# First block's mixing stage: rope on GpSimd, the first long tile's scores evicted by ScalarE, one mask add for all heads

## The chip, the cores and the metric

The kernel runs on one NeuronCore of a Trainium2 chip. The metric is the device time of one execution in microseconds (us). The core's engines take their instructions in order, each from its own queue, and wait for one another through semaphores: TensorE (PE in the profile, its weight loads PEld), VectorE (DVE), ScalarE (ACT), GpSimd (POOL) and SyncE (SP, which issues the DMAs here).

## The reference

Two blocks of two layers each run one after the other. Only the first block is touched. Its residual has 272 positions (16 learned ones and 256 tokens) of width 1024, all in float32. One layer of it is

```
z = x @ w_in                            # 4176 columns
q,k,v -> causal conv of width 4, silu -> gated delta rule, 4 heads of 128
sq,sk,iq,ik = rope(...)                 # rope(x) = x*cos + rot(x)*sin
score = sum_h relu(iq_h . ik / 8) * wi_h, causal     # 8 heads of 64
keep  = the best 64 positions of each row by score
p = softmax(sq_h . sk_h / 8 where kept, else -inf);  o_h = p @ sv_h
x = layer_norm(alpha*x + [delta, sparse] @ w_out);  then a mixture of experts
```

## The kernel before

Activations lie transposed: features on the 128 partitions, the 272 positions along the free axis. For the attention, the queries are cut into tiles of 16, 128 and 128 rows (`TILES`); tile 1 sees 144 keys, tile 2 sees 272. Softmax with kept positions only is made by adding a mask `bias` that is 0 or -1e30.

`mixers` builds one layer's mixing stage out of three parts: `projections` (35 groups of matmuls, the conv and the rope), `delta_rule` (three chunks of 16, 128 and 128 positions; a chunk's triangular inverse goes through up to six levels, each a round from TensorE over ScalarE and VectorE back) and `sparse_attention`. Each part is a generator for each engine, and it yields a planned time ahead of each step. `interleave` merges the three generators of an engine by these planned times. So the planned times (`projection_time`, `DELTA_START`, `RANK_START`, `ATTEND_START`) fix the order of the instructions on each engine and nothing else; the engines then run that order with semaphore waits. Planned times are not microseconds of the profile.

In words, the steps that the change touches:

- **Rope.** ScalarE copies a projection out of its bank (line 278) into `ikT` (1 group of 272 columns), `iqT`, `sqT` and `skT` (4 groups each). When a tensor is whole, `swap(r)` on SyncE issues four DMAs (line 211) that write the halves swapped into `rope_tmp`, which lies in the room of `xT` and is shown by that name. VectorE then does three passes: `swapped *= sin` (317), `x *= cos` (319), `x += swapped` (322), and counts `rope_out`. The next swap waits for it. TensorE waits for `rope_out` 2 ahead of the first ranking matmul (719) and for 4 ahead of the first attention score (737).
- **Ranking.** For each tile, eight heads go from TensorE (719) through a relu on ScalarE (792) to an accumulation on VectorE (845, 847). Then VectorE finds the best 64 in eight rounds (857, 859) and makes the mask (862, 864).
- **Attention.** For each tile TensorE writes head h's scores (737) to bank 6 or 7, in turn. VectorE takes them out, scaled and masked, into `lg` (881, `s_logit_sb`), and head h+2 waits for that. `lg` and the tile `rel` lie in the fourth weight slot and are shown as `W`. Then come the row maxima (884), exponentials (802), sums and probabilities (812), transposes (769) and products with `sv` (778). Between tile 1's scores and its transposes the 16 short rows are done (743, 748, 754).
- **Value projections.** Groups 28, 29 and 30 (line 248, 8 matmuls of 512 columns each) make `sv`; ScalarE copies them out (282).
- **Delta rule, chunk 2 (the third), around the scores.** TensorE: 440, 442 (products of keys and queries, counted by `d_kk`), 447, 449 (transposes, waiting for VectorE's `d_LA` behind 623 to 628); the levels are 456 (LX) and 463, 466 (YP, PY), answered by 538 on ScalarE and 647, 651, 654 on VectorE. Chunk 1 runs the same lines as much as five levels ahead of chunk 2.

Of the kernel before, what the change touches and what calls it, by code (L numbers as in the profile page):

```python
# [9 lines left out]
ALU = mybir.AluOpType  # L10
# [3 lines left out]
P = 128  # L14
# [5 lines left out]
T = SEQ + N_META  # L20
# [106 lines left out]
def projection_time(n):  # L127

    if n < 12:
        return 4.0 * n  # L130
    if n < 15:
        return 48.0 + 2.0 * (n - 12)
    if n < 28:
        return 54.0 + 4.0 * (n - 15)
    if n < 31:
        return 112.0 + 12.0 * (n - 28)
    return 150.0 + 9.0 * (n - 31)


def projections(nc, m, l, A, S):  # L140
# [147 lines left out]
    def on_vector(dve):  # L288
        yield 0
        dve.wait_ge(S["params_turned"], 1)  # L290
        nc.vector.tensor_copy(m.prmT[:, 0:81], ps[7][:, 0:81])
        dve.drain().then_inc(S["params_copied"], 1)
        for n, (kind, chunk, c0, idx) in enumerate(plan):
            if kind == "conv":
                yield projection_time(n) + 4.2
                dve.wait_ge(S["proj_by_act"], idx + 1)
                if idx >= 2:
                    dve.wait_ge(S["conv_silu"], idx - 1)
                y = m.conv_out[:, idx % 2, :]
                for j in range(4):  # L300
                    x = m.xpad[:, idx % 3, j:j + T]
                    wj = m.prmT[:, 12 * j + idx:12 * j + idx + 1]
                    if j == 0:
                        i = nc.vector.tensor_scalar(y, x, wj, None, ALU.mult)
                    else:
                        i = nc.vector.scalar_tensor_tensor(y, x, wj, y, ALU.mult, ALU.add)
                    if j < 3:
                        dve.drain()
                i.then_inc(S["conv"], 1)
            elif kind == "rope" and idx in (0, 4, 8, 12):  # L310
                yield projection_time(n) + 7.0
                r = idx // 4
                x, landed = turned[r]
                w = x.shape[1]
                swapped = m.rope_tmp[:, 0:w, :]
                dve.wait_ge(S["rope_swapped"], 64 * (r + 1))
                nc.vector.tensor_tensor(swapped, swapped, m.sin[:, :].unsqueeze(1).to_broadcast([P, w, T]), ALU.mult)
                yield projection_time(n) + 8.0
                nc.vector.tensor_tensor(x, x, m.cos[:, :].unsqueeze(1).to_broadcast([P, w, T]), ALU.mult)
                yield projection_time(n) + 9.0  # L320
                dve.drain()
                nc.vector.tensor_tensor(x, x, swapped, ALU.add)
                dve.drain().then_inc(S["rope_out"], 1)
            elif kind == "bai":
                yield projection_time(n) + 2.0
                dve.wait_ge(S["proj"], n + 1)
                nt = TILES[idx][1]
                nc.vector.tensor_copy(m.bai[0:nt, idx, :], ps[n % 2][0:nt, 0:16])
                dve.drain().then_inc(S["proj_by_dve"], 1)

    return on_sync, on_tensor, on_scalar, on_vector


DELTA_START = (62.0, 73.0, 104.0)
# [334 lines left out]


RANK_START = {1: 80.0, 2: 97.3}
ATTEND_START = {1: 115.0, 2: 155.0}


def sparse_attention(nc, m, S, ctx):
# [27 lines left out]
    def turn_bank(a, h):  # L703

        return ps[0] if a and h % 2 else ps[6]

    def on_tensor(pe):
        for c in (1, 2):
            t0, n = TILES[c]
            ns = t0 + n  # L710
            for h in range(NH):
                q = (c - 1) * NH + h
                yield RANK_START[c] + 1.2 * h
                if q == 0:
                    pe.wait_ge(S["rope_out"], 2)
                    pe.wait_ge(S["d_ln"], 6)
                if q >= 2:
                    pe.wait_ge(S["s_rel"], q - 1)
                nc.tensor.matmul(ps[6 + h % 2][0:n, 0:ns], m.iqT[half(h), h // 2, t0:t0 + n], m.ikT[half(h), 0:ns],
                                 start=True, stop=True).then_inc(S["s_idx"], 1)  # L720
        for c in (1, 2):
            t0, n = TILES[c]
            ns = t0 + n
            at = ATTEND_START[c]
            a = c - 1
            for h in range(NH):
                q = a * NH + h
                yield at + h
                if q == 0:
                    pe.wait_ge(S["rope_out"], 4)  # L730
                    pe.wait_ge(S["s_rel"], 2 * NH)
                if a and h < 2:
                    pe.wait_ge(S["s_pT_sb"], NH)
                    pe.wait_ge(S["s_out"], 1)
                if h >= 2:
                    pe.wait_ge(S["s_logit_sb"], q - 1)
                nc.tensor.matmul(ps[6 + h % 2][0:n, 0:ns], m.sqT[half(h), h // 2, t0:t0 + n], m.skT[half(h), h // 2, 0:ns],
                                 start=True, stop=True).then_inc(S["s_logit"], 1)
            if a == 0:
                yield at + 9.5  # L740
                pe.wait_ge(S["s_logit_sb"], NH)
                for h in range(NH):
                    mm = nc.tensor.matmul(ps[6 + h % 2][0:M, h // 2 * M:h // 2 * M + M], m.sqT[half(h), h // 2, 0:M], m.skT[half(h), h // 2, 0:M], start=True, stop=True)
                mm.then_inc(S["s_short_logit"], 1)
                yield at + 17
                pe.wait_ge(S["s_short_prob"], 1)
                for h in range(NH):
                    mm = nc.tensor.transpose(ps[6][0:M, M * h:M * h + M], short[:, 0, h, :], m.ident[0:M, 0:M])
                mm.then_inc(S["s_short_pT"], 1)
                yield at + 19  # L750
                pe.wait_ge(S["proj_by_act"], 12 + 13 + 1)
                pe.wait_ge(S["s_short_pT_sb"], 1)
                for h in range(NH):
                    mm = nc.tensor.matmul(ps[7][half(h), h // 2 * M:h // 2 * M + M], m.sv[0:M, 0, h * 64:(h + 1) * 64], short[:, 1, h, :], start=True, stop=True)
                mm.then_inc(S["s_short_pv"], 1)
            for h in range(NH):
                q = a * NH + h
                yield at + 23 + 2.2 * h
                if h == 0:
                    pe.wait_ge(S["s_prob"], a + 1)  # L760
                if a == 0 and h:
                    pe.wait_ge(S["s_pT_sb"], q)
                if a and h == 1:
                    pe.wait_ge(S["proj_by_act"], 12 + 13 + 3 + 4)
                if a and h >= 2:
                    pe.wait_ge(S["s_pT_sb"], q - 1)
                for j in range(c + 1):
                    s0, w = TILES[j]
                    mm = nc.tensor.transpose(turn_bank(a, h)[0:w, j * P:j * P + n], lg[0:n, h, s0:s0 + w], m.ident[0:n, 0:n])
                mm.then_inc(S["s_pT"], 1)  # L770
                yield at + 24.5 + 2.2 * h
                if q == 0:
                    pe.wait_ge(S["proj_by_act"], 12 + 13 + 3)
                    pe.wait_ge(S["s_short_out"], 1)
                pe.wait_ge(S["s_pT_sb"], q + 1)
                for j in range(c + 1):
                    w = TILES[j][1]
                    mm = nc.tensor.matmul(ps[7][half(h), h // 2 * P:h // 2 * P + n], m.sv[0:w, j, h * 64:(h + 1) * 64],
                                          pT[0:w, h % 2, j, 0:n], start=(j == 0), stop=(j == c))
                mm.then_inc(S["s_pv"], 1)  # L780

    def on_scalar(act):
# [10 lines left out]
        for c in (1, 2):  # L793
            t0, n = TILES[c]
            ns = t0 + n
            at = ATTEND_START[c]
            a = c - 1
            yield at + 11
            act.wait_ge(S["s_max"], a + 1)
            for h in range(NH):  # L800
# [31 lines left out]
    def on_vector(dve):  # L832
# [36 lines left out]
        for c in (1, 2):  # L869
# [2 lines left out]
            at = ATTEND_START[c]  # L872
            a = c - 1
            mask = bias[0:n, a, 0:ns]
            for h in range(NH):
                q = a * NH + h
                yield at + h + 0.6
                if a and h == 0:
                    dve.wait_ge(S["s_pT"], NH)
                dve.wait_ge(S["s_logit"], q + 1)  # L880
                nc.vector.scalar_tensor_tensor(lg[0:n, h, 0:ns], ps[6 + h % 2][0:n, 0:ns], 0.125, mask, ALU.mult, ALU.add).then_inc(S["s_logit_sb"], 1)
            yield at + 9
            dve.drain()
            nc.vector.tensor_reduce(mx[0:n, :], lg[0:n, :, 0:ns], AX.X, ALU.max)
            dve.drain()
# [30 lines left out]
def interleave(*streams):  # L916


    for _ in together(streams):
        pass  # L920
# [11 lines left out]
def mixers(nc, m, l, A, S):  # L932

    with ExitStack() as ctx:
# [3 lines left out]
        with nc.Block() as block:  # L938
# [12 lines left out]
            @block.vector  # L951
            def _(dve):
                interleave(project[3](dve), linear[2](dve), sparse[2](dve))


def layer_norm_steps(nc, m, signals, banks, g0, b0):
# [2200 lines left out]
```

## Time and profile before

| | us |
|---|---|
| three runs | 2714.68, 2725.06, 2725.97; median 2725.06 |
| profiled execution, its own time | 2709.52 |
| its span | 2707.7 |
| mean granted TensorE clock | 0.937 of full speed |
| mixing stage, layer 0 | about 25 to 322 of the span |
| mixing stage, layer 1 | about 685 to 978 of the span |

In the profile, a line of the timeline gives the start, the time taken, the engine, the line of the kernel, and the tensors written and read; in brackets stand the idle time of the engine ahead of it and who ended that. A float32 matmul is shown as two records or more, so `x16` is eight matmuls. Tensors with a common first word (`d`) are the work tensors of the delta rule.

### The profile page before, as it was taken

To read this page: it belongs to the slowest core of one execution; us is meant where nothing else is said; L and a number is where in the kernel's file an instruction comes from. 1 tells how busy PE (TensorE), PEld (TensorE's weight loads), DVE (VectorE), ACT (ScalarE), POOL (GpSimd) and SP (SyncE) were. 2 spreads that over 40 slices of the span, in tenths; PEclk is the share of its full clock that TensorE was granted. 3 is DMA by queue.
4 is the path that set the end of the run, shared out by engine and by line. 5 is a ranking of instruction groups with operands and counts; after the bars stand their busy time and mean duration, and the time that the engine had idled before them with its cause. 6 is when DMAs were issued, how large, how long until landed. Compare 5 with 4: busy or idle time off the path is not lost. (4 is left out here: it accounts for less than half of the span.)

```text
span 2707.7 us, 32418 instructions
## 1 busy us (share of the span) xinstructions
PE 2377.2 (88%) x12008; PEld 1751.5 (65%) x12008; DVE 844.9 (31%) x1901; ACT 529.7 (20%) x1178; POOL 0.2 (0%) x4
## 2 busy tenths in 40 slices
PE   8888878787998887888599799999989979999998
PEld 6656664333765665443376577778877657777887
DVE  3473233223356313222334422311112432231112
ACT  2212320101311322101232331110002233111000
POOL 0000000000000000000000000000000000000000
PEclk9889879999988996999899899999999989999999
DMA  6220227997321031999654042333434404233342
GB/s 208 73 79 32 88 100 300 402 394 299 107 81 40 32 144 72 394 407 395 255 168 161 0 156 79 129 135 127 153 111 138 154 0 156 83 131 129 131 148 109
DMA packets 165151, 426.40 MB, mean 157 GB/s; under 512 B 40409, under 2 KB 54294, under 8 KB 140454
## 3 DMA queue, kind: packets, MB, share of 16 engines
q1 hardware_dynamic: 165030, 424.80, 42.7%
q8 instruction: 75, 1.23, 0.2%
q14 instruction: 46, 0.38, 0.0%
HBM read 419.06 MB, written 1.05 MB: 155 GB/s over the span
## 5 line engine op out<-in xcount | busy, mean ns | idle before, releaser
L1928 PE MATMUL bank<-hT,W 128*128 128x256 f32 (+1 forms) x1440 | 329.7, 384 | 5.9 <-issue 2.6
L1928 PEld LDWEIGHTS bank<-hT,W 128*128 128x128 f32 (+1 forms) x1440 | 267.6, 189 | 54.6 <-issue 14.2
L253 PE MATMUL bank<-hT,W 128*128 128x272 f32 x928 | 246.2, 425 | 18.0 <-issue 12.3
L2906 PE MATMUL bank<-hT,W 128*128 128x256 f32 x1024 | 228.8, 384 | 13.8 <-issue 7.0
L253 PEld LDWEIGHTS bank<-hT,W 128*128 128x128 f32 x928 | 190.3, 208 | 64.6 <-issue 22.4
L2923 PE MATMUL bank<-u_hid,W 128*128 128x256 f32 x1024 | 225.1, 380 | 6.5 <-issue 6.5
L2906 PEld LDWEIGHTS bank<-hT,W 128*128 128x128 f32 x1024 | 195.6, 192 | 46.7 <-issue 20.0
L2923 PEld LDWEIGHTS bank<-u_hid,W 128*128 128x128 f32 x1024 | 193.2, 190 | 38.4 <-issue 12.7
L1320 PE MATMUL bank<-W,e_hs 128*32 128x512 f32 x1024 | 140.6, 711 | 56.4 <-DMA W<-in_w 54.7
L1299 PE MATMUL bank<-e_sel,rowsH 128*128 128x128 f32 (+1 forms) x768 | 149.2, 328 | 17.9 <-DVEq L1416 10.1
L1299 PEld LDWEIGHTS bank<-e_sel,rowsH 128*128 128x128 f32 (+1 forms) x768 | 113.9, 204 | 61.3 <-issue 25.4
L1320 PEld LDWEIGHTS bank<-W,e_hs 128*32 128x32 f32 x1024 | 41.4, 127 | 154.4 <-issue 154.4
L2983 DVE TENSOR_TENSOR xT<-xT,bank 128x256 f32<-128x256 f32 x128 | 53.9, 421 | 177.1 <-PE bank L2923 177.1
L1310 PE MATMUL bank<-e_back,e_y 128*128 128x272 f32 x288 | 84.5, 415 | 18.5 <-DVE yT L1435 13.0
L2952 ACT ACTIVATE u_hid<-u_rel 128x256 f32<-128x256 f32 x64 | 26.6, 416 | 363.0 <-DVEq L2977 363.0
L2975 DVE SCALAR_TENSOR_TENSOR u_rel<-bank,rstd 128x256 f32<-128x256 f32 x64 | 27.2, 425 | 217.0 <-PE bank L2906 187.1
L1310 PEld LDWEIGHTS bank<-e_back,e_y 128*128 128x128 f32 x288 | 45.6, 188 | 53.1 <-DVE yT L1435 41.0
L1439 DVE TENSOR_TENSOR e_hid<-e_sil,bank 128x256 f32<-128x256 f32 x16 | 9.6, 600 | 198.4 <-ACTq L1385 198.4
L1062 PE MATMUL bank<-mixT,W 128*128 128x272 f32 x256 | 64.9, 410 | 1.9 <-PEq L938 1.9
L1435 DVE TENSOR_TENSOR yT<-yT,bank 128x272 f32<-128x272 f32 x128 | 54.5, 436 | 23.2 <-PE bank L1310 19.4
L1062 PEld LDWEIGHTS bank<-mixT,W 128*128 128x128 f32 x256 | 51.1, 200 | 13.7 <-issue 2.6
L1340 PE MATMUL bank<-e_Wd,e_hidT 128*32 128x512 f32 x512 | 58.2, 595 | 0.0
(538 smaller groups left out, 2888.9 us busy)
## 6 DMA issues: line engine op xcount, KB each, us to landing
W<-in_w SPq DMA_DIRECT2D x128, 1024.0 KB, 10.2
W<-in_w_in SPq DMA_DIRECT2D x41, 2048.0 KB, 8.2
e_Wd<-in_w SPq DMA_DIRECT2D x64, 1024.0 KB, 9.0
W<-in_w_up SPq DMA_DIRECT2D x16, 2048.0 KB, 9.0
W<-in_w_down SPq DMA_DIRECT2D x16, 2048.0 KB, 7.9
W<-in_w_out SPq DMA_DIRECT2D x8, 2048.0 KB, 8.0
W<-in_mem_w_kv SPq DMA_DIRECT2D x6, 2048.0 KB, 10.9
W<-in_cmp_w SPq DMA_DIRECT2D x4, 2048.0 KB, 8.4
```

The source lines that it names most:

```text
L253: mm = nc.tensor.matmul(bank[:, 0:T], w[:, k, c0:c0 + P], m.hT[:, k, :], **st)
L1062: mm = nc.tensor.matmul(ps[n % 4][:, 0:T], w[:, k, n % 4 * P:n % 4 * P + P], m.mixT[:, k, :], start=(k == 0), stop=(k == KT - 1))
L1299: mm = nc.tensor.matmul(o, m.rowsH[0:nt, c, d * P:(d + 1) * P], sel[0:nt, c, :], start=(c == 0), stop=(c == 2))
L1310: nc.tensor.matmul(ps[6 + d % 2][:, 0:T], y[:, d * P:(d + 1) * P], back[:, 0, :], start=True, stop=True).then_inc(S["e_part"], 1)
L1320: mm = nc.tensor.matmul(ps[2][32 * j:32 * j + 32, :], hs[:, k, 32 * j:32 * j + 32], Wu[:, j, :, k, :], start=(k == 0), stop=(k == KT - 1))
L1340: mm = nc.tensor.matmul(ps[4 + h][32 * j:32 * j + 32, :], hidT[:, f, 32 * j:32 * j + 32], Wd[:, j, f * D + 512 * h:f * D + 512 * h + 512], ...
L1435: nc.vector.tensor_tensor(m.yT[:, d, :], m.yT[:, d, :], ps[6 + d % 2][:, 0:T], ALU.add).then_inc(S["e_y_free"], 1)
L1928: mm = nc.tensor.matmul(o[0:n, 0:S2], w[:, k, a:a + n], m.hT[:, k, :], start=(k == 0), stop=(k == KT - 1))
L2906: mm = nc.tensor.matmul(ps[j][:, 0:S2], w[:, k, j * P:(j + 1) * P], m.hT[:, k, :], start=(k == 0), stop=(k == KT - 1))
L2923: mm = nc.tensor.matmul(ps[4 + n % 2][:, 0:S2], w[:, k, n * P:(n + 1) * P], hid[:, x, k, :], start=(k == 0), stop=(k == 3))
L2975: nc.vector.scalar_tensor_tensor(rel[:, j, :], ps[j][:, 0:S2], 0.0, m.rstd[:, :], ALU.max, ALU.mult)
L2983: nc.vector.tensor_tensor(m.xT[:, n, :], m.xT[:, n, :], ps[4 + n % 2][:, 0:S2], ALU.add).then_inc(S["u_y_free"], 1)
```

## The change

The three rope passes move from VectorE's stream to GpSimd, which had no instruction in this stage; the waits and the counts are the same. For tile 1, ScalarE takes the scores out of the banks with the scale alone, and VectorE adds the mask once, in place, for all eight heads. Tile 2 keeps the old way. Planned times move: tile 1's scores are half a unit apart in place of one unit and start at 113.5 in place of 115, and with them all later steps of tile 1 come 1.5 earlier; `sv` groups 28, 29 and 30 go from 112, 124, 136 to 111, 120.5, 130.

```diff
     if n < 31:
-        return 112.0 + 12.0 * (n - 28)
+        return 111.0 + 9.5 * (n - 28)
...
-            elif kind == "rope" and idx in (0, 4, 8, 12):
-                yield projection_time(n) + 7.0
...
-                dve.wait_ge(S["rope_swapped"], 64 * (r + 1))
-                nc.vector.tensor_tensor(swapped, swapped, m.sin[:, :].unsqueeze(1).to_broadcast([P, w, T]), ALU.mult)
-                yield projection_time(n) + 8.0
-                nc.vector.tensor_tensor(x, x, m.cos[:, :].unsqueeze(1).to_broadcast([P, w, T]), ALU.mult)
-                yield projection_time(n) + 9.0
-                dve.drain()
-                nc.vector.tensor_tensor(x, x, swapped, ALU.add)
-                dve.drain().then_inc(S["rope_out"], 1)
...
+    def on_gpsimd(pool):
+        for r, (x, _) in enumerate(turned):
+            w = x.shape[1]
+            swapped = m.rope_tmp[:, 0:w, :]
+            pool.wait_ge(S["rope_swapped"], 64 * (r + 1))
+            nc.gpsimd.tensor_tensor(swapped, swapped, m.sin[:, :].unsqueeze(1).to_broadcast([P, w, T]), ALU.mult)
+            nc.gpsimd.tensor_tensor(x, x, m.cos[:, :].unsqueeze(1).to_broadcast([P, w, T]), ALU.mult)
+            pool.drain()
+            nc.gpsimd.tensor_tensor(x, x, swapped, ALU.add)
+            pool.drain().then_inc(S["rope_out"], 1)
...
-ATTEND_START = {1: 115.0, 2: 155.0}
+ATTEND_START = {1: 113.5, 2: 155.0}
...
+        return 1.0 if a else 0.5          # pace(a)
...
-                yield at + h
+                yield at + pace(a) * h
...
+            if a == 0:
+                for h in range(NH):
+                    yield at + pace(a) * h + 0.3
+                    act.wait_ge(S["s_logit"], h + 1)
+                    i = nc.scalar.activation(lg[0:n, h, 0:ns], ps[6 + h % 2][0:n, 0:ns], ACT.Copy, scale=0.125)
+                    i.then_inc(S["s_logit_sb"], 1)
...
+            if a == 0:
+                yield at + 5
+                dve.wait_ge(S["s_logit_sb"], NH)
+                nc.vector.tensor_tensor(lg[0:n, :, 0:ns], lg[0:n, :, 0:ns], mask.unsqueeze(1).to_broadcast([n, NH, ns]), ALU.add)
+            else:
...
-            yield at + 9
+            yield at + 9 - 3 * (a == 0)
```

Merged by planned time, TensorE's order around tile 1's scores is, before: LX3 of chunk 1, `sv` 28, 440/442 of chunk 2, PY3 of chunk 1, scores 0 to 2, 447/449 of chunk 2, score 3, LX4 of chunk 1, scores 4 to 7, LX1 of chunk 2, PY4 of chunk 1, `sv` 29, short scores (743), PY1 of chunk 2, LX5 of chunk 1, LX2 of chunk 2, 748, PY5, 754, `sv` 30, PY2 of chunk 2, LX6 of chunk 1, first transpose (769), first product (778). After: LX3, `sv` 28, 440/442, scores 0 and 1, PY3, scores 2 to 7, 447/449, LX4, `sv` 29, LX1 of chunk 2, short scores, PY4, PY1 of chunk 2, LX5, `sv` 30, 748, LX2 of chunk 2, PY5, 754, PY2 of chunk 2, first transpose, LX6, first product. On ScalarE, the eight evictions stand ahead of 533 (chunk 2's copy behind 447/449), and the copy of `sv` 28 stands between the third and the fourth of them.

## Rows read from the trace of the kernel before

**Rows 1.** The page: busy time of the engines over the span.
```profile
PE 2377.2 (88%) x12008; PEld 1751.5 (65%) x12008; DVE 844.9 (31%) x1901; ACT 529.7 (20%) x1178; POOL 0.2 (0%) x4
```

**Rows 2.** Windows: span, busy time of PE, PEld, DVE, ACT, POOL, then PEclk.
```profile
190.00:201.00 11.00, 0.94 (x8) 0.61 (x7) 9.79 (x25) 0.00 (x0) 0.00 (x0) 0.67 0.00 0
201.00:224.00 23.00, 22.17 (x106) 16.30 (x107) 11.45 (x25) 5.19 (x17) 0.00 (x0) 0.71 0.00 1
...
851.00:862.00 11.00, 3.05 (x11) 2.44 (x12) 8.83 (x21) 0.27 (x1) 0.00 (x0) 0.57 0.01 1
862.00:885.00 23.00, 21.30 (x129) 15.80 (x129) 13.16 (x28) 8.08 (x27) 0.00 (x0) 0.84 0.00 0
```

**Rows 3.** Timeline of TensorE, layer 0, around tile 1's scores.
```profile
120.17 0.52 PE L719 MATMUL bank<-ikT,iqT 64*128 64x144 f32 x4 [1.43 <-DVEq L323]
...
139.28 0.60 PE L449 MATMUL bank<-k_ident,d 128*128 128x128 f32 x4
...
187.42 1.06 PE L442 MATMUL bank<-qkvT 128*128 128x128 f32 x8
...
190.20 0.52 PE L737 MATMUL bank<-skT,sqT 64*128 64x144 f32 x4
200.77 0.84 PE L737 MATMUL bank<-skT,sqT 64*128 64x144 f32 x2 [10.05 <-DVE W L881]
...
212.46 1.91 PE L466 MATMUL bank<-d,d 128*128 128x128 f32 x8
214.17 7.07 PE L248 MATMUL bank<-W,hT 128*128 128x512 f32 x16
...
229.01 7.13 PE L248 MATMUL bank<-W,hT 128*128 128x512 f32 x16
...
241.20 0.79 PE L778 MATMUL bank<-W,sv 16*64 16x128 f32 x4 [1.66 <-ACT sv L282]
...
247.44 1.06 PE L466 MATMUL bank<-d,d 128*128 128x128 f32 x8
```

**Rows 4.** Timeline of VectorE, layer 0.
```profile
182.36 0.15 DVE L612 TENSOR_TENSOR d_egc<-d_egc,d_beta 128x4 f32<-128x4 f32 x1
...
184.67 0.69 DVE L620 TENSOR_TENSOR d<-qkvT,d 128x512 f32<-128x512 f32 x1
...
188.72 1.29 DVE L322 TENSOR_TENSOR skT<-skT,xT 128x1088 f32<-128x1088 f32 x1
...
196.26 0.69 DVE L623 TENSOR_TENSOR d<-bank,d 128x512 f32<-128x512 f32 x1
...
200.63 0.68 DVE L651 TENSOR_TENSOR d<-d,bank 128x512 f32<-128x512 f32 x1
...
281.07 2.42 DVE L884 TENSOR_REDUCE s_mx<-W 128x8 f32<-128x2176 f32 x1
```

**Rows 5.** Timeline of ScalarE, layer 0.
```profile
120.71 0.29 ACT L792 ACTIVATE W<-bank 128x144 f32<-128x144 f32 x1 [7.34 <-PE bank L719]
...
203.54 0.60 ACT L533 ACTIVATE d<-bank 128x512 f32<-128x512 f32 x1 [16.42 <-PE bank L449]
```

**Rows 6.** The swap's DMAs: SyncE's timeline, and times from issue to landing.
```profile
106.66 2.41 SPq L211 DMA_DIRECT2D xT<-iqT  x4
...
176.74 0.59 SPq L211 DMA_DIRECT2D xT<-skT  x1
...
DMA to landing us min/median/max: 2.3/2.4/2.4
```

**Rows 7.** Timeline of TensorE, layer 1.
```profile
848.51 0.52 PE L737 MATMUL bank<-skT,sqT 64*128 64x144 f32 x4
...
898.04 0.79 PE L778 MATMUL bank<-W,sv 16*64 16x128 f32 x4 [1.66 <-ACT sv L282]
```

More of the change, by code:

```diff
@@ L309, in on_vector @@
                 i.then_inc(S["conv"], 1)
-            elif kind == "rope" and idx in (0, 4, 8, 12):
-                yield projection_time(n) + 7.0
[L312 to L315, printed above, removed]
-                dve.wait_ge(S["rope_swapped"], 64 * (r + 1))
-                nc.vector.tensor_tensor(swapped, swapped, m.sin[:, :].unsqueeze(1).to_broadcast([P, w, T]), ALU.mult)
-                yield projection_time(n) + 8.0
-                nc.vector.tensor_tensor(x, x, m.cos[:, :].unsqueeze(1).to_broadcast([P, w, T]), ALU.mult)
-                yield projection_time(n) + 9.0
-                dve.drain()
-                nc.vector.tensor_tensor(x, x, swapped, ALU.add)
-                dve.drain().then_inc(S["rope_out"], 1)
             elif kind == "bai":
@@ L329, in on_vector @@
                 dve.drain().then_inc(S["proj_by_dve"], 1)
-    return on_sync, on_tensor, on_scalar, on_vector
+    def on_gpsimd(pool):
[8 more added lines that the diff above has]
+            pool.drain().then_inc(S["rope_out"], 1)
+    return on_sync, on_tensor, on_scalar, on_vector, on_gpsimd
 DELTA_START = (62.0, 73.0, 104.0)
@@ L705, in turn_bank, with pace @@
         return ps[0] if a and h % 2 else ps[6]
+    def pace(a):
+        return 1.0 if a else 0.5
     def on_tensor(pe):
@@ L874, in on_vector @@
             mask = bias[0:n, a, 0:ns]
[L875 to L881, printed above, removed]
-            yield at + 9
+            if a == 0:
[3 more added lines that the diff above has]
+            else:
+                for h in range(NH):
+                    q = a * NH + h
+                    yield at + h + 0.6
+                    if h == 0:
+                        dve.wait_ge(S["s_pT"], NH)
+                    dve.wait_ge(S["s_logit"], q + 1)
+                    nc.vector.scalar_tensor_tensor(lg[0:n, h, 0:ns], ps[6 + h % 2][0:n, 0:ns], 0.125, mask, ALU.mult, ALU.add).then_inc(S["s_logit_sb"], 1)
+            yield at + 9 - 3 * (a == 0)
             dve.drain()
@@ L953, in _ @@
                 interleave(project[3](dve), linear[2](dve), sparse[2](dve))
+            @block.gpsimd
+            def _(pool):
+                project[4](pool)
 def layer_norm_steps(nc, m, signals, banks, g0, b0):
```

## Prediction

> **What bounds the kernel now.** I read the page first. TensorE is busy for 88% of the span, VectorE for 31%, GpSimd not at all [rows 1]. An edit off TensorE is therefore worth only what it takes out of TensorE's waits or gives back in its clock. Next I read the windows over the mixing stage for a stretch in which TensorE is not busy. There is one in each layer: of the 11 us from 190 to 201 TensorE works 0.94 while VectorE works 9.79, and at 851 to 862 it is 3.05 against 8.83 [rows 2]. Then I read the timelines of the two engines. TensorE issues tile 1's scores 0 and 1 at 190.20 and idles 10.05 us, until VectorE has taken the first out of its bank [rows 3]. ScalarE idles 16.42 us over the same stretch [rows 5]. VectorE is not waiting at all: it has just made the last rope pass on `skT` at 188.72, works off the ranking rounds of tile 2 and chunk 2's products from 196.26 on, and reaches the first eviction just ahead of the 651 at 200.63 [rows 4]. So the bound there is VectorE's queue, and what stands ahead of the eviction in it.
>
> Then the clock. After the gap the granted clock is 0.71 of full speed over 201 to 224, and 0.84 in layer 1 [rows 2]; the eight matmuls of 466 take 1.91 us at 212.46 and 1.06 at 247.44 [rows 3], the 1.2 GHz level against the 2.4 one. The matmuls from 200.77 to 214.17 fill 13.4 us with 0.6 of idle time; at the full clock they would need about half of it, so the gap costs another 6.4 us behind it.
>
> **What the change takes out of VectorE.** Three passes of 1.29 us [rows 4] for each of `iqT`, `sqT` and `skT`, and three short ones for `ikT`. Between 177 and 196, where it matters, these are 3 x 1.29 = 3.87 us. Eight evictions go and one add of 1152 elements comes; by 1.29 for 1088 it takes 1.36 us, and it stands behind chunk 2's 633 and chunk 1's 651, where TensorE no longer waits for it. On ScalarE eight evictions come, 0.29 us each as the relu of the same shape [rows 5], into its 16.42 idle us: free, if the scores come as planned. If they come late, ScalarE waits with the copy of `sv` 28 and with 533 behind it.
>
> **What GpSimd needs.** No instruction like these is in the trace. From below, a pass costs what VectorE needs, 1.29 us. From above, I let the two inputs and the output go one after the other, 3 x 1.29 = 3.87. In between is an engine that reads its inputs one after the other, 2176 elements; the nearest row is a VectorE instruction over 2176 elements at 2.42 us [rows 4]. I take 2.42, the one in the middle. With 0.4 for the drains and semaphores, three passes are 7.7 us.
>
> The Trainium skill (GPSIMD Engine Reference, section 3.1, Elementwise) states about 2.6 cycles an element on this engine, because its two inputs share one read port, and 4497 ns for 2048 elements; scaled to 1088 that is an estimate of 2.39 us a pass, and no run here shows it yet.
>
> Where it is needed: the last DMA of `skT` is issued at 176.74 and lands 2.4 later, 179.1 [rows 6]; rope ends at 186.8. TensorE comes to the first score when 442 ends, 187.42 + 1.06 = 188.5 [rows 3]: no wait, 1.7 to spare. For `iqT` the four issues end at 109.1, the last starts 0.6 before that and lands at 110.9 [rows 6]; rope ends at 118.6. TensorE now starts at 120.17 behind a wait of 1.43 for this rope [rows 3], so up to 1.4 is gained, at 3.87 a pass 2.8 is lost. I take 0.5. For `sqT` nobody waits before 188. The swaps stay on SyncE, and only its next swap waits for `rope_out`, with more than ten us to spare.
>
> **VectorE beside GpSimd.** The trace can't show whether they hinder each other. From below: nothing. From above: VectorE loses as much as it saved, 3.87. TensorE and ScalarE work on the same memory beside VectorE in all these rows, and its passes keep their 1.29 and 0.69 us; so I stay below the middle and take 1.5.
>
> The Trainium skill (SBUF — State Buffer, section Who interferes with whom) says that the second port pair is an exclusive lock: a VectorE instruction with two SBUF inputs and a GpSimd instruction that reads SBUF exclude each other for whole instructions. By that rule 612 and 620 [rows 4] would each wait out the rest of a pass, and so up to some 2 x 2.4 us would go from the 3.87; the sum below would lose up to 3 us a layer. It is the rule that speaks most against this change.
>
> **The stretch replayed, layer 0**, in the new order, from 188.5:
> - scores 0 and 1 (0.6) and PY3 (2 x 1.0) to 191.0; scores 2 to 7, two banks in turn, each round a matmul, an eviction of 0.29 and two semaphores, about 1.0 a pair: to 193.9.
> - 447/449 wait for VectorE. Its 623 starts at 196.26 - 3.87 + 1.5 = 193.9, 628 ends 2.7 behind it: 196.6. They take 2 x 0.60 [rows 3]: 197.8.
> - LX4 waits for 651, now right behind 633: 193.9 + 4.2 + 0.8 = 198.9. It ends at 199.9.
> - `sv` 29: 7.1 [rows 3], to 207.0. LX1 1.0, PY4 and PY1 2.0 each, short scores 0.4: 212.4. LX5 1.0, `sv` 30 7.1: 220.5. LX2, PY5, PY2, LX6: 6.0, and four short steps with 1.8 less the 0.4 already counted: 227.9, the first product of 778.
>
> Before, this product starts at 241.20, behind a wait of 1.66 for the copy of `sv` 30, which stands right ahead of it in the old order [rows 3]; in the new order it is seven steps back. The gain is 13.3. The later pairs of transpose and product lie closer together and wait for ScalarE's copy in between somewhat more, 0.8 at most: 12.5 left. What comes behind (tile 2, chunk 2's end, the output projection, the experts' DMAs issued as the stage ends) waits on nothing with a time of its own, and shifts whole.
>
> **The clock in the new order** is the largest unknown. From 191 to 199 TensorE still idles some 4 us. From below the loss is 0, from above the 6.4 of before. I take half, 3.2: 9.3 in layer 0.
>
> Layer 1 has the same pattern, 898.04 - 848.51 = 49.5 us from first score to first product [rows 7] against 51.0 in layer 0, since the clock took less. So 1.5 less: 7.8. With 2 x 0.5 from `iqT`: 9.3 + 7.8 + 1.0 = **18.1 us**. Against the profiled execution (span 2707.7, time 2709.5, nothing of weight outside it) that is 2691.4. The median of the runs lies 15.5 higher, at 2725.06; the edit saves the same there: **2707 us**.
>
> **Rivals.**
> 1. *The forecast*: GpSimd stays ahead of TensorE, the gap shrinks from 10 to some 4 us, the clock loss at most halves or goes. From 2695 (no clock loss, nothing between VectorE and GpSimd, all of `iqT`'s wait: 15 a layer) to 2711. Chance 0.66.
> 2. *GpSimd near the upper bound, or VectorE shut out beside it.* At 3.87 a pass `iqT` costs 2.8; VectorE at the upper bound, 2.4 more than taken; 3.2 for the clock: 12.5 - 2.8 - 2.4 - 3.2 = 4.1, less 1.5 in layer 1, so 7 us in all, 2718. For: no row bounds it better. Against: the passes are plain streams. Chance 0.15.
> 3. *The gap closes, but the time isn't kept*: the clock falls as low and as long as before (12.5 - 6.4 = 6, 5 in layer 1), or tile 1 comes earlier than chunk 2, whose chain of levels then sets the end. Some 9 us, 2716. For: clock rows vary between the layers for the same work. Against: TensorE has few waits after 224. Chance 0.08.
> 4. *Slower*: GpSimd's passes become TensorE's bound. TensorE is in order: a late `rope_out` holds the delta rule's levels behind it too. A pass of X ends `iqT` at 111.3 + 3X against 120.1, and `skT` at 179.5 + 3X, which reaches LX4 6.7 later against 198.9. Both losses together eat the 9.3 at X = 5.1. At 6 us a pass it is 9.2 + 5.3 - 9.3 = 5 a layer, with layer 1 some 12: 2737. For: the engine has not one row. Against: 5 us is four times VectorE's pass. Chance 0.11.
>
> A measurement of this kernel tells 0.5%, 13.6 us, from no change, so faster means below 2711.4: 0.66, the first case. Within: 0.23. Slower: 0.11. The range, 2692 to 2720, takes in the first three cases and the spread of single runs; it leaves out the slower case and some tails.
>
> **What would show it.** GpSimd's three passes on 1088 columns each, near 2.4 us; the first 719 no later than 120.2; the wait ahead of the third score gone, and the longest idle stretch near it ended by 628 or 651; the first 778 near 228 to 231 and in layer 1 near 888; VectorE's 623 at 192.4 (nothing lost), 193.9 or 196. The prediction is wrong if passes take over 3.5 us, if 616 to 620 grow gaps of whole passes, or if the clock rows over 191 to 210 stay at the lower level.

## Result, and the profile after

| | before | after |
|---|---|---|
| timed runs, median (us) | 2722.94 (4 runs, 2714.68 to 2725.97) | 2691.52 (4 runs, 2686.26 to 2693.21) |
| profiled execution, span (us) | 2707.7 | 2689.5 |
| mean granted clock | 0.937 | 0.937 |

The ratio is 0.9886, with a 95% interval of 0.9859 to 0.9913: 31 us faster. Between the two profiled executions the difference is only 18.2 us. The forecast was 18.1 us, and 2691.4 us for the profiled execution, which took 2691.51. But the forecast for the runs' median was 2707, and the measured 2691.5 lies just under the range of 2692 to 2720. So the question is where the other 13 us are. One execution of the kernel before, in r1_before_again, took 4078.84 us at a granted clock of 0.55; it is in none of the medians and ratios here.

In the changed kernel the lines have moved: 719 is now 720, 737 is 738, 447/449 are 444/446, 456 is 453, 463/466 are 460/463, 623 to 633 are 620 to 630, 647 is 644, 612 is 609, 620 is 617, 651 is 648 and 778 is 779. New are 803 (ScalarE's eviction), 885 (the mask add) and 322, 323, 325 (rope).

The page of the changed kernel, busy time of the engines:

```profile
PE 2379.8 (88%) x12008; PEld 1751.7 (65%) x12008; DVE 836.3 (31%) x1863; ACT 533.6 (20%) x1194; POOL 54.4 (2%) x28
```

GpSimd's timeline in layer 0: one of the short passes on `ikT`, one of the long ones on `iqT`, and those on `skT`.

```profile
88.31 1.81 POOL L323 TENSOR_TENSOR ikT<-ikT,k_cos 128x272 f32<-128x272 f32 x1
...
118.66 2.50 POOL L325 TENSOR_TENSOR iqT<-iqT,xT 128x1088 f32<-128x1088 f32 x1
...
181.98 2.48 POOL L322 TENSOR_TENSOR xT<-xT,k_sin 128x1088 f32<-128x1088 f32 x1 [25.65 <-DMA xT<-skT]
184.42 2.49 POOL L323 TENSOR_TENSOR skT<-skT,k_cos 128x1088 f32<-128x1088 f32 x1
187.05 2.75 POOL L325 TENSOR_TENSOR skT<-skT,xT 128x1088 f32<-128x1088 f32 x1
```

A long pass takes 2.48 us (2.42 was taken), and 2.75 where it meets VectorE. Rope on `skT` is done at 189.8, 0.9 us ahead of the first score, where the forecast had 1.7 to spare. TensorE's timeline, answering [rows 3]:

```profile
92.50 0.20 PE L424 MATMUL bank<-d_gate,k_cum 16*16 16x4 f32 x2 [1.91 <-DVEq L595]
...
122.54 0.52 PE L720 MATMUL bank<-ikT,iqT 64*128 64x144 f32 x4
...
190.70 0.52 PE L738 MATMUL bank<-skT,sqT 64*128 64x144 f32 x4
...
194.01 2.03 PE L738 MATMUL bank<-skT,sqT 64*128 64x144 f32 x8 [0.37 <-ACT W L803]
198.42 1.12 PE L444 MATMUL bank<-k_ident,d 128*128 128x128 f32 x4 [2.37 <-DVEq L626]
...
200.59 2.08 PE L453 MATMUL bank<-d,d 128*128 128x128 f32 x8 [0.21 <-DVEq L649]
202.46 7.22 PE L248 MATMUL bank<-W,hT 128*128 128x512 f32 x16
...
215.37 7.03 PE L248 MATMUL bank<-W,hT 128*128 128x512 f32 x16
...
229.33 0.79 PE L779 MATMUL bank<-W,sv 16*64 16x128 f32 x4
```

The wait of 10.05 us is gone. What is left of it are 0.37, 2.37 and 0.21. From the first score to the first product it is 38.6 us in place of 51.0, although PY3 (2 us) now lies inside that stretch. The first product waits for nothing. But the first ranking matmul comes 103.3 us behind the stage's first projection, at 19.2, in place of 101.2 behind 19.0. In layer 1 it is 100.9 in place of 100.7.

VectorE's timeline, answering [rows 4]:

```profile
87.63 1.87 DVE L576 SCALAR_TENSOR_TENSOR qkvT<-qkvT,d_sq 128x1088 f32<-128x1088 f32 x1 [7.29 <-ACT d_sq L507]
89.42 1.84 DVE L577 TENSOR_TENSOR qkvT<-qkvT,d_sq 128x1088 f32<-128x1088 f32 x1
...
116.94 1.65 DVE L644 TENSOR_TENSOR d<-d,k_levelsT 16x64 f32<-16x64 f32 x1
...
183.46 1.02 DVE L609 TENSOR_TENSOR d_egc<-d_egc,d_beta 128x4 f32<-128x4 f32 x1
184.40 0.15 DVE L610 COPY d_etot<-d 128x4 f32<-128x4 f32 x1
184.63 0.69 DVE L613 TENSOR_TENSOR d<-bank,d_egc 128x512 f32<-128x512 f32 x1
...
186.63 0.82 DVE L617 TENSOR_TENSOR d<-qkvT,d 128x512 f32<-128x512 f32 x1
...
195.68 0.69 DVE L620 TENSOR_TENSOR d<-bank,d 128x512 f32<-128x512 f32 x1
...
201.43 1.36 DVE L885 TENSOR_TENSOR W<-W,s_bias 128x1152 f32<-128x1152 f32 x1
```

An instruction over 64 elements takes 1.65 us in place of 0.21 beside a pass of GpSimd, and 609 takes 1.02 in place of 0.15. Those that read a bank (613) keep their 0.69. The mask add takes 1.36, as worked out.

**Both stages laid side by side.** "Stage" is from the first projection (line 253) to the first output projection (1062) of a layer. All times are starts in TensorE's timeline.

| us | stage 0 | between | stage 1 | behind | span |
|---|---|---|---|---|---|
| before, first profile | 303.8 | 358.2 | 297.6 | 1729.1 | 2707.7 |
| after | 292.7 | 360.9 | 286.8 | 1729.9 | 2689.5 |

The stages became 11.1 and 10.8 us shorter, 21.9 together; 3.7 went the other way outside of them (2.7 between the stages, 0.8 behind them, 0.2 ahead), where the kernels are the same.

### The profile page after: what moved, and what is told of

It is laid out like the page before. It is cut to its first block and busy times, and to the rows that moved or that the text cites. A ratio compares the mean times of both kernels' runs of the same rounds, so it can differ in the third digit from the quotient of the medians.

```text
span 2689.5 us, 32424 instructions
## 1 busy us (share of the span) xinstructions
PE 2379.8 (88%) x12008; PEld 1751.7 (65%) x12008; DVE 836.3 (31%) x1863; ACT 533.6 (20%) x1194; POOL 54.4 (2%) x28
## 5 line engine op out<-in xcount | busy, mean ns | idle before, releaser
L1944 PEld LDWEIGHTS bank<-hT,W 128*128 128x128 f32 (+1 forms) x1440 | 267.7, 189 | 54.7 <-issue 14.2
L253 PE MATMUL bank<-hT,W 128*128 128x272 f32 x928 | 248.8, 428 | 18.2 <-issue 12.3
L2922 PEld LDWEIGHTS bank<-hT,W 128*128 128x128 f32 x1024 | 194.4, 191 | 46.3 <-issue 20.2
L1315 PE MATMUL bank<-e_sel,rowsH 128*128 128x128 f32 (+1 forms) x768 | 149.2, 328 | 17.9 <-DVEq L1432 10.1
L1315 PEld LDWEIGHTS bank<-e_sel,rowsH 128*128 128x128 f32 (+1 forms) x768 | 113.9, 204 | 61.3 <-issue 25.3
L1326 PE MATMUL bank<-e_back,e_y 128*128 128x272 f32 x288 | 84.5, 415 | 18.9 <-DVE yT L1451 13.4
```

Of the source, the lines that this page charges most:

```text
L253: mm = nc.tensor.matmul(bank[:, 0:T], w[:, k, c0:c0 + P], m.hT[:, k, :], **st)
L1315: mm = nc.tensor.matmul(o, m.rowsH[0:nt, c, d * P:(d + 1) * P], sel[0:nt, c, :], start=(c == 0), stop=(c == 2))
L1326: nc.tensor.matmul(ps[6 + d % 2][:, 0:T], y[:, d * P:(d + 1) * P], back[:, 0, :], start=True, stop=True).then_inc(S["e_part"], 1)
L1944: mm = nc.tensor.matmul(o[0:n, 0:S2], w[:, k, a:a + n], m.hT[:, k, :], start=(k == 0), stop=(k == KT - 1))
L2922: mm = nc.tensor.matmul(ps[j][:, 0:S2], w[:, k, j * P:(j + 1) * P], m.hT[:, k, :], start=(k == 0), stop=(k == KT - 1))
```

## Experiments

Each kernel was profiled, and timed against the kernel before on the same chip. The table has what the comparisons rest on; "score to product" is from the first 737 to the first 778. "TensorE idle" is the length of a stage less TensorE's busy time in it, stage 0 and stage 1: an edit that removes waits shows there, and a change of the clock shows in the busy time.

| label | ratio to before (95%) | stage 0 | stage 1 | TensorE idle | score to product, layers 0 and 1 |
|---|---|---|---|---|---|
| first profile of before | | 303.8 | 297.6 | 38.9, 37.8 | 51.0, 49.5 |
| r1_before_again | 0.9996 (0.9984 to 1.0007) | 304.7 | 305.3 | 38.4, 37.9 | 51.1, 51.0 |
| r3_before_third | profile only | 305.4 | 305.2 | 38.4, 38.0 | 51.1, 51.0 |
| first profile of after | 0.9886 (0.9859 to 0.9913) | 292.7 | 286.8 | 26.2, 26.8 | 38.6, 38.8 |
| r2_after_again | 0.9888 (0.9872 to 0.9904) | 292.6 | 286.7 | 27.7, 26.8 | 39.2, 38.8 |
| e1_rope_only | 0.9954 (0.9941 to 0.9967) | 298.6 | 301.5 | 35.8, 35.6 | 47.7, 48.9 |
| e2_scores_only | 0.9910 (0.9897 to 0.9923) | 290.9 | 294.0 | 29.4, 30.2 | 40.3, 40.0 |
| e3_ikt_on_vector | 0.9849 (0.9831 to 0.9867) | 283.6 | 288.1 | 24.5, 23.9 | 38.5, 38.5 |
| e4_order_only | 0.9952 (0.9936 to 0.9969) | 299.2 | 298.4 | 34.5, 34.3 | 46.2, 46.3 |
| e5_old_order | 0.9928 (0.9912 to 0.9945) | 296.4 | 294.5 | 32.3, 33.0 | 41.6, 43.0 |
| e6_more_gpsimd | 0.9927 (0.9910 to 0.9945) | 295.8 | 294.5 | 35.5, 35.0 | 46.1, 46.1 |
| e7_before_shifted | 1.0007 (0.9990 to 1.0023) | 300.2 | 302.7 | 37.6, 37.6 | 49.3, 50.8 |
| e8_after_shifted | 0.9917 (0.9892 to 0.9942) | 289.6 | 292.4 | 25.9, 25.8 | 38.4, 38.4 |
| e9_products_first | 0.9843 (0.9822 to 0.9863) | 284.2 | 284.4 | 24.6, 25.3 | 38.0, 38.1 |

The change takes idle time out of both stages, 12.2 and 11.1 us against r1_before_again, and 10 to 13 whichever profiles are compared. TensorE's busy time, for the same matmuls, differs by up to 8.3 us between the profiles, in both directions, and that is what makes the stage lengths hard to read. The comparisons ran on three chips (r1, r2, e1 and e2 on one, e3 to e6 on the second, e7 to e9 and r3 on the third); which chip took the first two profiles isn't on record.

### r1_before_again, r3_before_third: the kernel before, unchanged

> The kernel before, unchanged, once more profiled and timed. Theory A (the profiled execution of before was a fast one of a varying kernel, 2709.5 against 2714.7 to 2726.0 in its runs): this profile shows a span nearer 2718 and the extra time can be found in it. Rival B (profiled executions of before are always faster than its timed ones): span again near 2708 with timed runs near 2722. Ratio to before 1.000 either way.

> The kernel before, profiled a third time. Theory (the first profile caught a rare fast second stage): span near 2720, second mixing stage near 305 us with more time at the lower clock than in the first profile. Rival (both are as common): span near 2708, second stage near 298.

Measured: spans of 2722.0 and 2719.2 us, timed runs of r1_before_again with a median of 2722.02. The first profile, 2709.5 us, was below every timed run of the kernel before, in the later comparisons (from 2714.8 up) and in r1_before_again's own (from 2712.4 up). Theory A holds. Of the 14.3 us between the spans of the first profile and r1_before_again 7.7 lie in stage 1, 0.9 in stage 0, 2.2 between the stages and 3.5 elsewhere; only stage 1 is looked into here. Windows of stage 1, and of the part of it from the first ranking matmul to the first score; behind the length stand the busy times of PE, PEld, DVE, ACT and POOL, then the granted clock, the DMA share and GB/s. First the first profile of before:

```profile
681.00:978.60 297.60, 259.76 (x1397) 194.82 (x1398) 134.17 (x293) 83.42 (x206) 0.00 (x0) 0.91 0.19 59
...
781.70:848.50 66.80, 63.73 (x324) 45.54 (x324) 43.52 (x98) 12.48 (x36) 0.00 (x0) 0.92 0.26 80
```

The same of r1_before_again:

```profile
684.40:989.70 305.30, 267.36 (x1398) 202.12 (x1398) 134.20 (x293) 83.36 (x206) 0.00 (x0) 0.89 0.18 57
786.40:856.50 70.10, 67.03 (x326) 48.36 (x326) 43.45 (x98) 12.46 (x36) 0.00 (x0) 0.88 0.24 76
```

The stage is 7.7 us longer, and TensorE's busy time is 7.6 longer, for the same 1398 records (one is missing from the first trace); VectorE's and ScalarE's busy times are the same. So no wait is added: the same matmuls take longer, at a clock of 0.89 in place of 0.91. r3_before_third has 305.2 us at 0.89, on another chip. The timed runs lean the same way: the two shortest spans of r1_before_again, 2710.6 and 2710.7, have a granted clock of 0.935, its two longest, 2723.6 and 2724.3, have 0.931.

### r2_after_again: the changed kernel, unchanged

> The changed kernel, unchanged. Theory A: spans between 2684 and 2692 again, ratio 0.987 to 0.990, since its runs spread over 7 us only. Rival (the 31 us of the first comparison were chance, the true saving is the 18.2 of the two profiles): ratio 0.993.

Measured: 0.9888, span 2689.1, stages within 0.1 us of the first profile. The saving of the runs is 30 us, not 18. The equal length of stage 0 is in part chance: TensorE is 1.6 us less busy in it than in the first profile, and 1.5 us more idle.

### e7_before_shifted, e8_after_shifted: the stage begins later

```diff
     def on_tensor(pe):
         last_chunk = None
+        pe.wait_ge(S["shifted"], 1)
...
     def on_vector(dve):
+        for _ in range(4):
+            nc.vector.memset(m.conv_out[:, :, :], 0.0)
+            i = dve.drain()
+        i.then_inc(S["shifted"], 1)
```

> The kernel before with one thing added: at the start of each mixing stage VectorE clears its conv buffer four times and TensorE waits for that, which moves the whole stage some 2 to 3 us and changes nothing inside it. Theory (how long TensorE stays at the lower clock inside a stage depends on when the stage's sparse stretches fall, so one kernel's stage takes 297.6 or 305.3 us): the lengths of the two stages from their first projection differ from 303.8 and 305.3 by more than 2 us in one or both, and the windows with the longer times have the lower granted clock. Rival (the stage's length is fixed by its waits): both within 1 us of 304.5.

> The changed kernel with the same 2 to 3 us added ahead of each mixing stage. Theory: its stages, 292.7 and 286.8 us from the first projection on, change by more than 2 us in one or both, by the clock; the total is anywhere from 0.986 to 0.993. Rival: 292.7 and 286.8 within 1 us, total 4 to 6 us above the changed kernel, 0.991.

Measured, for before: the stages take 300.2 and 302.7 us in place of 304.7 to 305.4 in r1_before_again and r3_before_third (the first profile had 303.8 and 297.6). TensorE's idle time stays within 0.8 us of r1's, and its busy time falls. The granted clock is 0.91 in stage 0, where it was 0.90 and 0.89, and 0.89 in stage 1 as before, so the expected sign, a lower clock with the longer time, shows in stage 0 alone. For the changed kernel: 289.6 and 292.4 in place of 292.7 and 286.8, so 3.1 less and 5.6 more. The windows over the changed kernel's stage 1, unshifted and then shifted:

```profile
672.80:959.60 286.80, 260.01 (x1398) 194.45 (x1398) 130.92 (x274) 85.59 (x214) 27.12 (x12) 0.92 0.20 61
```

```profile
674.20:966.60 292.40, 266.62 (x1398) 200.12 (x1398) 128.65 (x274) 85.27 (x214) 27.11 (x12) 0.89 0.19 60
```

The clock falls from 0.92 to 0.89, and TensorE's busy time grows by 6.6 us for the same records, while its idle time is 1.0 less. Nothing inside the stage was edited. So the rival, a length fixed by the waits, is out: a stage of this kernel takes some 6 us more or less by its granted clock. That it is the shift which moves the clock, by where the sparse stretches fall, fits but isn't shown: there is one profile of each shifted kernel, and the kernel before moved by 7.7 us without any shift. In the unshifted changed kernel stage 1 has the better clock, in two profiles of two.

### e1_rope_only, e2_scores_only, e4_order_only, e5_old_order: the parts

e1_rope_only has the rope as in the change, and evictions and planned times as before. e2_scores_only is the changed kernel with the rope passes back in VectorE's stream. e4_order_only is the kernel before with

```diff
-        return 112.0 + 12.0 * (n - 28)
+        return 111.0 + 9.5 * (n - 28)
...
-ATTEND_START = {1: 115.0, 2: 155.0}
+ATTEND_START = {1: 113.5, 2: 155.0}
...
-                yield at + h + 0.6
+                yield at + (1.0 if a else 0.5) * h + 0.6
```

the same pace on TensorE, and tile 1's later steps on VectorE 3 units earlier. e5_old_order is the changed kernel with the planned times of before.

> The rope on GpSimd, nothing else: scores of tile 1 still leave their banks through VectorE, old planned times. Theory (what frees TensorE is the eviction by ScalarE, since the eviction stands behind the ranking rounds in VectorE's queue): the wait ahead of the third score stays near 8 us (10.05 less 3.87 given up, plus some 2 of exclusion), ratio 0.997 to 1.001. Rival (VectorE's load is what counts, so the rope alone gives most of it): wait under 5 us, ratio below 0.993.

> Everything of the change but the rope, which stays on VectorE. Theory (the eviction and the new order carry the gain): the third score no longer waits, chunk 2's transposes (447, 449) wait instead until VectorE's 628, some 2 to 4 us later than in the changed kernel, and nothing is lost ahead of the stage to GpSimd; ratio 0.988 to 0.992. Rival (without the rope gone VectorE is as late as before and the wait only moves to 447, 449): ratio 0.996 to 0.999.

> Only the planned times of the change; VectorE still takes tile 1's scores out and does the rope. Theory (the eviction stands behind the ranking rounds in VectorE's queue whatever the plan says): TensorE waits about 8 to 10 us ahead of the third score as before, the copies of sv no longer stall the first product; ratio 0.996 to 1.000. Rival (the plan alone, which fills the wait with the value projections, gives the gain): ratio below 0.993.

> Rope on GpSimd, tile 1's scores through ScalarE and one mask add, but with the planned times of before (sv at 112, 124, 136, scores one unit apart from 115). Theory (the eviction is what counts, the new order adds the 1.7 us stall of the first product and some of the waits filled by the value projections): ratio 0.990 to 0.993. Rival (without the new order the gain is gone, TensorE then waits between the scores for VectorE's 628): ratio above 0.995.

Measured: 0.9954, 0.9910, 0.9952 and 0.9928. For e2_scores_only and e5_old_order the theory's range held, though not all that was said of the waits: in e2_scores_only 447 comes 1.2 us later against the first score than in the changed kernel, not 2 to 4 (its own wait is 3.55 us), and the first score waits 1.51 us for the rope. For e1_rope_only and e4_order_only neither range did; both fell between theory and rival (e4's interval reaches into the theory's). TensorE's waits show why. In e1_rope_only the wait ahead of the third score is 7.02 us; the expected 8 allowed 2 us for VectorE being held up by GpSimd, and 10.05 - 3.87 = 6.18 leaves 0.8:

```profile
194.99 0.85 PE L734 MATMUL bank<-skT,sqT 64*128 64x144 f32 x2 [7.02 <-DVE W L878]
```

In e4_order_only the wait is split, and 1.6 us of it now are for the rope, which the earlier scores meet unfinished:

```profile
191.56 0.52 PE L737 MATMUL bank<-skT,sqT 64*128 64x144 f32 x4 [1.60 <-DVEq L323]
198.09 0.51 PE L737 MATMUL bank<-skT,sqT 64*128 64x144 f32 x2 [4.03 <-DVE W L881]
202.44 1.06 PE L737 MATMUL bank<-skT,sqT 64*128 64x144 f32 x4 [3.85 <-DVE W L881]
```

It gains because the value projections come earlier and the stall of the first product, 1.66 us, goes; score to product falls from 51 to 46. In e5_old_order the scores no longer wait for their bank, but chunk 2's transposes stand between score 2 and score 3 and wait 4.55 us for VectorE, and the first product stalls again:

```profile
198.16 1.11 PE L444 MATMUL bank<-k_ident,d 128*128 128x128 f32 x4 [4.55 <-DVEq L626]
...
233.82 0.79 PE L779 MATMUL bank<-W,sv 16*64 16x128 f32 x4 [1.66 <-ACT sv L282]
```

So three steps share the gain: eviction by ScalarE with the plan 24 us (e2), with the rope but without the plan 20 (e5), the plan alone 13 and the rope alone 12.5, all three 30. They overlap: each takes something off the same wait. The idle time of TensorE tells them apart without the clock. Against r1_before_again it falls, in the two stages, by 2.6 and 2.3 us for the rope alone, 3.9 and 3.6 for the plan alone, 9.0 and 7.8 for eviction with the plan, 6.1 and 4.9 for eviction with the rope, and 12.2 and 11.1 for all three. So the rope passes on GpSimd add about 3 us a stage to the other two; in the ratios (0.9910 and 0.9888) the intervals overlap. Eviction alone wasn't run, nor the rope with the plan.

### e3_ikt_on_vector: the short rope goes back

```diff
+            elif kind == "rope" and idx == 0:
...                                           # the three passes, as before
-        for r, (x, _) in enumerate(turned):
+        for r, (x, _) in list(enumerate(turned))[1:]:
```

> The changed kernel with the short rope on ikT back on VectorE; the three long ones stay on GpSimd. Theory (GpSimd's passes on ikT fall on VectorE's 579 and 580 and stretch them, which makes TensorE's wait for chunk 0's start 1.9 in place of 0.8 us): the first ranking matmul comes 1 to 2 us earlier against the stage's start, 579 and 580 are 1.29 us again, ratio 0.0005 to 0.001 below the changed kernel's 0.989. Rival (the later start is the granted clock's, not GpSimd's): 579 and 580 shorter, but the ranking no earlier.

Measured: 0.9849, about 11 us less than the changed kernel, four times the most that was expected. The instructions that the expectation calls 579 and 580 (576 and 577 in the changed kernel, 590 and 591 here) are 1.29 us again, and TensorE waits 0.76 us in place of 1.91:

```profile
86.68 1.29 DVE L590 SCALAR_TENSOR_TENSOR qkvT<-qkvT,d_sq 128x1088 f32<-128x1088 f32 x1 [7.02 <-ACT d_sq L521]
87.89 1.28 DVE L591 TENSOR_TENSOR qkvT<-qkvT,d_sq 128x1088 f32<-128x1088 f32 x1
```

```profile
90.41 0.20 PE L438 MATMUL bank<-d_gate,k_cum 16*16 16x4 f32 x2 [0.76 <-DVEq L609]
```

That is the 1.15 us that the theory stands for, and in layer 1 it is 1.09 (1.84 to 0.75). The start of ranking doesn't show it, though: against the stage's start it comes 3.7 us earlier in layer 0 and at the same 100.9 us in layer 1, where 2.5 us less idle time are made up for by 2.5 more of busy time. Stage 0 is 9.1 us shorter and stage 1 is 1.3 longer. The windows from the first ranking matmul to the first score of layer 0, of the changed kernel and then of this one:

```profile
122.50:190.70 68.20, 65.18 (x314) 46.57 (x310) 42.02 (x95) 11.88 (x35) 15.54 (x6) 0.87 0.25 78
```

```profile
119.40:182.80 63.40, 60.36 (x314) 42.85 (x310) 42.21 (x96) 11.89 (x35) 15.56 (x6) 0.95 0.27 84
```

Same records, 4.8 us less, all of it TensorE's busy time, at 0.95 in place of 0.87. Over the whole stages TensorE's idle time falls by 1.7 and 2.9 us; its busy time falls by 7.4 in stage 0 and grows by 4.2 in stage 1. So 4.6 us of the gain are waits, more than expected, and the larger part of stage 0's gain is the clock again.

### e6_more_gpsimd: GpSimd works on beside VectorE

```diff
             pool.drain().then_inc(S["rope_out"], 1)
+        for _ in range(5):
+            nc.gpsimd.tensor_tensor(m.rope_tmp[:, :, :], m.rope_tmp[:, :, :], m.sin[:, :].unsqueeze(1).to_broadcast([P, 4, T]), ALU.mult)
+            pool.drain()
```

> The changed kernel with five more passes of the same size on GpSimd behind the last rope, on a buffer that nobody reads any more; no result changes and nobody waits for them but the stage's end. They lie beside VectorE's 623 to 641. Theory (GpSimd and VectorE exclude each other for whole instructions when VectorE reads two tensors from SBUF): VectorE's 627, 628, 631, 633 take up to 2.5 us in place of 0.69, TensorE's 447 starts 3 to 6 us later against the first score, and the ratio rises by 0.002 to 0.005 to 0.991 to 0.994. Rival (no exclusion, long rows of VectorE beside GpSimd have another cause): no change against the changed kernel, 0.989.

Measured: 0.9927, inside the theory's range, though other instructions paid, and more of it: the passes ended at 198.4, just ahead of 623, and met 647 and the mask, and 447 came 7.6 us later against the first score where 3 to 6 were expected. VectorE's timeline:

```profile
185.29 0.09 DVE L869 MATCH_VALUE_LOAD s_work<-s_top,s_work 128x8 f32 x1
185.37 0.43 DVE L869 MATCH_REPLACE8 s_work<-s_top,s_work 128x272 f32<-128x272 f32 x1
185.87 2.36 DVE L647 TENSOR_TENSOR d<-d,k_levelsT 128x512 f32<-128x512 f32 x1
...
191.44 2.06 DVE L872 SCALAR_TENSOR_TENSOR s_keep<-s_work,k_causal 128x272 f32<-128x272 f32 x1
193.57 2.42 DVE L874 TENSOR_SCALAR s_bias<-s_keep 128x272 f32<-128x272 f32 x1
196.06 2.40 DVE L877 TENSOR_SCALAR s_short_bias<-k_causal 16x16 f32<-16x16 f32 x1
```

Four instructions that take 0.69, 0.44, 0.30 and 0.16 us in the changed kernel take 2.36, 2.06, 2.42 and 2.40 here: each waits out a pass. The ranking rounds (`max8` and `match_replace8`) keep 0.44 and 0.43. TensorE's wait ahead of 447 grows from 2.37 to 9.96 us. By the lock of the Trainium skill (SBUF — State Buffer, section Who interferes with whom) that is how it should be, for two inputs in SBUF (the memory that holds the tensors other than the banks), and for `tensor_scalar` in its modes that use two ports. The trace agrees, with 2.36 and 2.06 us for the first kind and 2.42 and 2.40 for the second; which mode those two ran in, no trace shows. The prediction's own bound, nothing to 3.87 us, held no such case: with GpSimd busy throughout, the wait grew by 7.6 us, TensorE's idle time by 9.3 and 8.2, and the stages by 3.1 and 7.7.

### e9_products_first: chunk 2's products ahead of the last ranking rounds

```diff
-                yield at + 10.6 + 0.8 * r
+                yield at + 10.6 + (0.8 if c == 1 else 1.4) * r
...
-            yield at + 17.1
+            yield at + (17.1 if c == 1 else 21)
```

on top of e3_ikt_on_vector.

> A candidate: the changed kernel with ikT's rope on VectorE, and the eight ranking rounds of tile 2 spread in VectorE's plan (1.4 apart in place of 0.8, the mask at 21 in place of 17.1), so that chunk 2's products 623 to 628 run as soon as TensorE has made them, ahead of the last three rounds. Theory (what TensorE still waits for is VectorE's 628 behind the ranking): the wait of some 2.4 us ahead of 447 goes, each stage 2 to 4 us shorter, ratio 0.982 to 0.984 against 0.985 without it. Rival (the wait only moves to the row maxima or to 651): ratio 0.984 to 0.986.

Measured: 0.9843, in the rival's range of 0.984 to 0.986 and just above the theory's, with an interval that takes in both; span 2676.7. The wait ahead of 447 (here 458) is gone, and half of it stands ahead of LX4 (456, here 467):

```profile
189.97 0.85 PE L458 MATMUL bank<-k_ident,d 128*128 128x128 f32 x4
...
193.00 2.08 PE L467 MATMUL bank<-d,d 128*128 128x128 f32 x8 [1.33 <-DVEq L663]
```

TensorE's idle time is 24.6 and 25.3 us, no less than the 24.5 and 23.9 of e3_ikt_on_vector. So the wait has moved, as the rival says, and nothing shows that this order is worth anything by itself. Both kernels are faster than before and than the changed kernel of r2_after_again; their intervals don't tell them from one another.

## Why the prediction was right in one frame and wrong in the other

**The mechanism held.** VectorE's queue was the bound, ScalarE's evictions cost TensorE a wait of 0.37 us, GpSimd stayed ahead of TensorE, and 11 to 12 us of TensorE's idle time went in each stage.

**That 18.2 us met the 18.1 worked out is luck.** The stages of the two profiles differ by 21.9, and 3.7 went back in stretches that the edit doesn't touch. Within layer 0, too, misses cancel: up to the end of 442 2.1 us were lost where a gain of 0.5 was taken; from there to the first product 14.2 were gained where the sum has 10.1 (13.3 less 3.2 for the clock); behind it 1.0 was lost, 0.8 taken.

**GpSimd's pass**: 2.42 taken, 2.48 measured, 2.75 and 2.94 where it met VectorE. The bound of 3.87 was never near. The estimate of 2.39 by the Trainium skill (GPSIMD Engine Reference, section 3.1, Elementwise) was as good, and the trace agrees.

**VectorE beside GpSimd**: 1.5 taken. Before, 623 starts 7.8 us behind the end of 442 (187.42 + 1.06 to 196.26, [rows 3, 4]); after, 4.9 (190.77 to 195.68). So 2.9 of the 3.87 saved were kept and 1.0 lost, in 612 and 620 as named. Whole passes were waited out earlier in the stage, beside `sqT` (3.00 us for one of 0.69), where TensorE had no wait for it.

**The replay**: 447 forecast 8.1 us behind the end of 442, measured 7.7; LX4 10.4 against 9.8; the first product 39.4 without any clock loss, measured 38.6 with it. The steps were too long together by more than the clock took. Of the 3.2 us for the clock some 2 were used, by 444, 446 and 453 at the lower level; the granted clock over 190.7 to 200 is 0.79, over 200 to 211 it is 0.87. (In the prediction's stretch of 13.4 us TensorE idles 0.83 us, not 0.6, which changes the 6.4 by 0.1.)

**`iqT`**: 0.5 a layer taken as gain. The wait of 1.43 went, but the start of ranking came 2.1 us later in stage 0, at 122.54 where the prediction said no later than 120.2. The prediction put no cost on GpSimd's passes on `ikT`: it did not see that they would meet 579 and 580, on which chunk 0's start waits. e3_ikt_on_vector shows 1.15 us of it. The rest is the clock: up to the start of ranking TensorE is busy 3.7 us more than before, at 0.92 in place of 0.95, and idle 1.6 less.

**What failed is the term of layer 1, 8.3 us with `iqT`, and with it the step from the profiled execution to the median**, "the edit saves the same there". The term is 10.8 against the first profile, and 18.5 against the kernel as it usually runs (305.3 less 286.8). The 49.5 us of [rows 7] and the 0.84 of [rows 2], from which it was made smaller than layer 0's, came from an execution whose stage 1 ran at a better clock than in both later profiles. Against r1_before_again the 32.5 us between the spans are 12.0 in stage 0, 18.5 in stage 1, -0.5 between the stages and 2.5 elsewhere. Of the 18.5, 11.1 are idle time (37.9 to 26.8) and 7.4 are TensorE's busy time for the same matmuls (267.4 to 260.0). In stage 0 the idle time falls by 12.2 and the busy time is as before (266.3 and 266.5). So the waits alone gave 12.2 and 11.1, more than the whole terms of 9.8 and 8.3. The 7.4 on top are the clock, which isn't bound to the edit: in e8_after_shifted, where nothing inside the stage was changed, stage 1 is busy for 266.6 us.

What stays open is what in the 723 to 856 us of the kernel before decides between the two clocks of stage 1. The start of the stage differs by 3.4 us between the profiles, which is about the size of the shift in e7 and e8, but with one profile of each the shift can't be told from chance. A difference between chips isn't excluded for the first profile either; r1 and r3, on two chips, agree.

## What to carry to other kernels

A profile is one execution: where the granted clock moves between executions, lay the profiled time beside the timed runs first, and when it lies outside of them, don't read a term of the sum from the stretch that makes the difference. Split the length of a stage into TensorE's idle and busy time: here the idle time of one kernel repeated within 1.5 us while its busy time moved by up to 7.6. An eviction that stands behind a long block in a full engine's queue is best given to an engine that idles there, and the planned order then has to put other TensorE work where the next wait moves. Elementwise work goes to GpSimd without harm only where VectorE reads a bank or runs `max8` and `match_replace8`; beside an instruction with two inputs in SBUF, or `tensor_scalar`, a pass can cost VectorE its own length.

## What the runs showed of the hardware

- GpSimd's `tensor_tensor` on 128 x 1088 float32 takes 2.48 us, 1.9 times VectorE's 1.29; on 128 x 272 it takes 0.76 us undisturbed. It waits for VectorE too: passes of 128 x 1088 took 2.75 and 2.94, one of 128 x 272 took 1.81.
- Beside it, VectorE's instructions with two SBUF inputs wait for the end of a pass (up to 3.00 us for one of 0.69, at 153.88 in the changed kernel), and so does `tensor_scalar` from SBUF down to 16 x 16 elements (2.40 for 0.16, in e6_more_gpsimd); `max8` (0.44), `match_replace8` (0.43) and those with one input in a bank (0.69) don't.
- The same 1398 records of TensorE filled 259.1 to 267.4 us in the profiles of this study, with granted clocks of 0.93 to 0.89. In the one kernel before, unchanged, stage 1 was busy for 259.8, 267.4 and 267.2 us.
